# Feed-forward products of a two-block transformer kernel: lower gated rows multiplied right behind their gate, sums of the down sets moved into the first product, left buffers assigned anew

## The reference, cut to what matters

```python
D_FF = 2816
def swiglu_ffn(x, w_gate, w_up, w_down):          # x: 512 x 1024
    return (jax.nn.silu(x @ w_gate) * (x @ w_up)) @ w_down

x = x + 0.5 * swiglu_ffn(rmsnorm(x, ffn1_norm[l]), ffn1_w_gate[l], ffn1_w_up[l], ffn1_w_down[l])
x = x + hybrid_mixer(...)
x = x + 0.5 * swiglu_ffn(rmsnorm(x, ffn2_norm[l]), ffn2_w_gate[l], ffn2_w_up[l], ffn2_w_down[l])
x = rmsnorm(x, final_norm[l])
```

## Time and profile before

| | us |
|---|---|
| median of 3 runs (lowest to highest) | 1792.81 (1790.96 to 1795.54) |
| the profiled execution | 1793.75 |
| its span | 1791.9 |
| TensorE busy | 1728.6 (96%) |
| VectorE busy | 1009.5 (56%) |
| ScalarE busy | 711.6 (40%) |

### The profile page before, as it was taken

One profiled execution on the slowest core, in us unless ns is written; L12 is line 12 of the kernel. 1 busy time (PEld: TensorE's weight loads), 2 busy tenths in 40 slices (PEclk: granted clock), 3 DMA queues, 4 the chain that ended last, 5 costly groups with the idle time before them and its releaser, 6 DMA issues.

```text
span 1791.9 us, 21492 instructions
## 1 busy us (share of the span) xinstructions
PE 1728.6 (96%) x8703; PEld 1282.3 (72%) x8703; DVE 1009.5 (56%) x1491; ACT 711.6 (40%) x1146; POOL 78.9 (4%) x78
## 2 busy tenths in 40 slices
PE   7999999989999999999999999999999999999997
PEld 6878888875545454544577887897877887887896
DVE  4768865642333232323558756755487557756755
ACT  4556335442111111111335455454355435455452
POOL 0000000000000000000011110100000001110100
PEclk9999999999999999999999999999999999999999
DMA  6222225557999999999838897873202267897871
GB/s 215 93 71 71 95 83 176 192 193 281 422 421 421 421 421 421 421 421 421 318 106 203 196 210 182 179 191 117 95 24 83 95 163 183 197 213 176 172 186 59
DMA packets 117513, 385.75 MB, mean 215 GB/s; under 512 B 7088, under 2 KB 22592, under 8 KB 91424
## 3 DMA queue, kind: packets, MB, share of 16 engines
q1 hardware_dynamic: 88928, 318.33, 46.3%
q0 software_dynamic: 26176, 61.78, 18.7%
q10 hardware_dynamic: 2304, 4.20, 0.6%
HBM read 364.36 MB, written 6.29 MB: 207 GB/s over the span
## 4 chain that ended last, share of the span: by engine, by line
PE 79%; DVE 12%; ACT 6%; issue 1%; DMA 1%; POOL 0%; SPq 0%; DVEq 0%; ACTq 0%
PE PS L1509 12%; PE PS L1621 6%; PE PS L1623 6%; PE PS L1622 6%; PE PS L1542 6%; PE PS L1656 5%; PE PS L1658 5%; PE PS L1657 5%; DVE lo L2412 4%; PE PS L1660 3%; PE PS L1662 3%; PE PS L1661 3%; ACT hi L1965 2%; PE PS L1480 2%; PE PS L1481 2%; PE PS L1552 2%
## 5 line engine op out<-in xcount | busy, mean ns | idle before, releaser
L2412 DVE TENSOR_TENSOR lo<-raw,hi 128x1024 fp32r<-128x1024 f32 (+2 forms) x275 | 332.0, 1225 | 247.3 <-ACT hi L1965 243.3
L1965 ACT CAST hi<-raw 128x1024 fp32r<-128x1024 f32 (+2 forms) x277 | 286.8, 1060 | 229.6 <-PE PS L1623 146.3
L1621 PE MATMUL PS<-hi,xh_ffn 128*128 128x512 f32 (+1 forms) x320 | 118.1, 369 | 0.0
L1623 PE MATMUL PS<-hi,xl_ffn 128*128 128x512 f32 (+1 forms) x320 | 117.5, 367 | 0.0
L1622 PE MATMUL PS<-lo,xh_ffn 128*128 128x512 f32 (+1 forms) x320 | 117.5, 367 | 0.0
L1509 PE MATMUL PS<-raw,XG 128*64 128x512 f32 x352 | 117.1, 593 | 0.0
L2372 DVE TENSOR_TENSOR HF<-SG,PS 128x512 f32<-128x512 f32 x16 | 17.4, 1090 | 165.5 <-PE PS L1509 165.5
L2387 DVE SCALAR_TENSOR_TENSOR YL<-PS,SM,YH 128x512 fp32r<-128x512 f32 x30 | 21.1, 747 | 138.8 <-ACT YH L1948 138.8
L2395 DVE TENSOR_TENSOR x_sb<-x_sb,PS 128x512 f32<-128x512 f32 x128 | 78.1, 678 | 8.7 <-PE PS L1553 8.7
L1931 ACT COPY HT<-PS 128x512 f32<-128x512 f32 x16 | 9.4, 586 | 175.1 <-PE PS L1518 175.1
L1660 PE MATMUL PS<-xTh,hi 128*128 128x512 f32 x192 | 78.3, 408 | 0.4 <-DVE lo L2412 0.3
(11 more groups left out here) (520 smaller groups left out, 4220.6 us busy)
## 6 DMA issues: line engine op xcount, KB each, us to landing
raw<-in_w_in SPq DMA_DIRECT2D x26, 1024.0 KB, 5.2
rawz<-in_w_down_experts SPq DMA_DIRECT2D x25, 1024.0 KB, 11.1
raw<-in_w_up_experts SPq DMA_DIRECT2D x24, 1024.0 KB, 15.5
raw<-in_w_gate_experts SPq DMA_DIRECT2D x20, 1024.0 KB, 15.8
raw<-in_ffn_w_down SPq DMA_DIRECT2D x20, 1024.0 KB, 7.6
rawz<-in_w_up_experts SPq DMA_DIRECT2D x19, 1024.0 KB, 19.5
raw<-in_w_down_experts SPq DMA_DIRECT2D x16, 1024.0 KB, 12.4
rawz<-in_w_gate_experts SPq DMA_DIRECT2D x16, 1024.0 KB, 14.2
```

What stands on the lines that cost most here:

```text
L1621: e.matmul(o, xh[:, k, c], h[:, k, :], start=k == 0 and not more, stop=False, skip_group_check=more)
L1623: x = e.matmul(o, xl[:, k, c], h[:, k, :], start=False, stop=k == 3, skip_group_check=more)
L1965: e.copy(q.hi[:, a:b], q.raw[:, a:b]).then_inc(*a_hi((u, 0) if part == 0 else u))
L2412: e.tensor_tensor(q.lo[:, a:b], q.raw[:, a:b], q.hi[:, a:b].bitcast(F32), ALU.subtract).then_inc(*v_lo(key))
```

## The change: what it does

There are three parts, all in the feed-forward layers.

1. "hb" stands at the end of `behind[5]`'s gate steps instead of behind product 6, so before the split of left operand A11 and before the weight splits that `feed.take` and `feed.split_first` add around product 6. "ht" stands before product 0 of the next set, and ahead of the turns of rows 2 and 3, instead of behind product 0; only the turns of rows 0 and 1 (`upper`) stay behind it. The same holds before the plain down product, where "ht" also goes ahead and the turns of rows 0 and 1 stay.
2. In a down set the split of S2 and the read-out of product 0 (`seven_x`) stand behind product 0, with the sums S1 and S2 that are there already; and the weight unit of product 2 is split there too, ahead of the turns of rows 0 and 1. A12, S1, A22, S4 keep their places behind products 1 to 4.
3. The left operands of products 0 to 6 lie in LB0, LB1, LB0, LB2, LB1, LB0, LB2 instead of LB0, LB1, LB2, LB0, LB1, LB2, LB0, and the waits of their rounding are changed to fit: A12 now waits for product 0, S1 for product 1, A22 for product 2, S4 for product 3, and S2 for nothing in its own set.

```diff
-        ahead = []
+        ahead, upper = [], []
         if past:
-            ahead = turns(*past, (2, 3))
-            behind[0] = gates("ht", past) + turns(*past, (0, 1))
+            ahead = gates("ht", past) + turns(*past, (2, 3))
+            upper = turns(*past, (0, 1))
         if what[0] == "gu":
             p, cut = what[1:]
-            own = {1: ("R1",), 2: ("C11",), 3: ("R2", "sg", "R0"), 4: ("C22",), 5: ("C21", "sgb"), 6: ("hb",)}
+            own = {1: ("R1",), 2: ("C11",), 3: ("R2", "sg", "R0"), 4: ("C22",), 5: ("C21", "sgb", "hb")}
...
             behind[0].extend([("sum", pre, p, "S1"), ("sum", pre, p, "S2")])
-            for j, ws in ((1, ("A12", "S2")), (2, ("S1",)), (3, ("A22",)), (4, ("S4",))):
-                for w in ws:
-                    behind[j].extend(split_left(pre, p, w))
-            for j, js in ((1, (1,)), (2, (0,)), (3, (3,)), (4, (4,)), (5, (5,)), (6, (2, 6))):
+            for j, w in ((0, "S2"), (1, "A12"), (2, "S1"), (3, "A22"), (4, "S4")):
+                behind[j].extend(split_left(pre, p, w))
+            for j, js in ((0, (0,)), (1, (1,)), (3, (3,)), (4, (4,)), (5, (5,)), (6, (2, 6))):
                 behind[j].extend(("seven_x", pre, p, q, t) for q in js for t in range(2))
...
             S.extend(behind[j])
+            if j == 0:
+                if what[0] == "s":
+                    feed.split_to(feed.taken + 2)
+                S.extend(upper)
...
         if ui == 0:
-            S.extend(turns(*past, (2, 3)))
+            S.extend(gates("ht", past) + turns(*past, (2, 3)))
...
             elif i == 3:
-                S.extend(gates("ht", past) + turns(*past, (0, 1)))
+                S.extend(turns(*past, (0, 1)))
...
-        LEFT_H = [LB[i] for i in (0, 1, 2, 0, 1, 2, 0)]
+        LEFT_H = [LB[i] for i in (0, 1, 0, 2, 1, 0, 2)]
...
-                    if j >= 3:
-                        act.wait_ge(p_mm, ((n, "s", p), j - 3, 1))
+                    if j in (2, 4, 5, 6):
+                        act.wait_ge(p_mm, ((n, "s", p), {2: 0, 4: 1, 5: 2, 6: 3}[j], 1))
                     elif p:
-                        act.wait_ge(p_mm, ((n, "s", p - 1), (6, 4, 5)[j], 1))
+                        act.wait_ge(p_mm, ((n, "s", p - 1), {0: 5, 1: 4, 3: 6}[j], 1))
```

## The result

| | before | after |
|---|---|---|
| median, us | 1794.12 (4 runs, 1790.96 to 1795.54) | 1771.57 (4 runs, 1770.76 to 1773.71) |
| ratio | | 0.9879, 95% interval 0.9861 to 0.9896 |
| profiled execution, its span | 1793.75, 1791.9 | 1771.79, 1770.0 |

The forecast was 1768.3, between 1762 and 1777. The measured gain is 22.5 us between the medians, the forecast one 24.6. Lines above 700 have moved by three: 1594 is now 1597, 1621 to 1623 are 1624 to 1626, 2412 is 2415, 2488 is 2491.

A forecast was written before the change was run, and what follows sets the result against it. TensorE, 96% busy, was taken as the bound, so only earlier starts count. Gains of 17.4 + 5.7 + 1.5 = 24.6 us gave 1768.3 us against the median 1792.81, with an 8-in-10 range of 1762 to 1777.

The forecast's parts named there:

- Into the down sets: Gate-up set followed by down set, four places: 26.1 us instead of 30.63 to product 4, 17.4 us gained together.
- The new wait of product 2: In each of four down sets, TensorE waits 2.2 us for A12's rest before product 2.
- between the ends I take no fall: Down sets: clock stays up after the 2.2 us wait; a fall would cost up to 7.2 us more in all.
- R1: Rival: the clock falls in the new wait before product 2 of the down sets; 1775.5 us, chance 0.14.
- no wait, with under 0.2 to spare: Down sets: product 4 starts without waiting for product 3's read-out, under 0.2 us to spare.
- My two reference points: Idle times before turns: 3.64 us followed by a clock fall, 1.64 us without; 2.2 taken as nearer the latter.
- Gate-up set into gate-up set: Four places where a gate-up set follows another: 1.43 us gained each, 5.7 us together.
- Into the plain down product: Two places before the plain down product: gain 1.24 less 0.5 lost on turned rows, 0.75 each, 1.5 us together.
- R2: Rival: no new wait at product 2 of the down sets; 1759.5 us, chance 0.09.
- R3: Rival: VectorE bounds the whole down set, bringing back read-out waits and some wait at product 2; 1774 us, chance 0.11.
- R4: Rival: sums by adding DMAs become the wait, at T2 for product 3 in down sets; 1796 us, chance 0.03.
- R5: Rival: TensorE finds another reason to wait at the turns and the time stays; 1793 us, chance 0.04.

The follow-up runs named there:

- e3: Against the kernel before: down-set order and left buffers as in the change, "hb" and "ht" not moved; 1790.54 us, ratio 0.9974.
- e2: Against the kernel before: only "hb" moved earlier, "ht" stays behind product 0 of the next set; 1767.19 us, ratio 0.9844.
- e0: The whole changed kernel run again, nothing altered; 1772.16 us, ratio 0.9869 against the kernel before.
- e6: e7 plus, before the plain down product, turned rows split ahead of "ht" and first down weights split by halves; 1759.00 us, ratio 0.9804.
- e1: Against the kernel before: only "hb" and "ht" moved earlier, down sets and left buffers as before; 1765.75 us, ratio 0.9836.
- e7: e1 with the sum S4 one product later, behind the read-out of product 3; 1761.83 us, ratio 0.9818.

## Why the prediction was right, point by point

**Into the down sets.** "hb" in VectorE's pause, turns at once, product 0 at full clock: all as worked out: 26.1 us were forecast to product 4, and 26.25 and 26.23 were measured at the two places without a fall. The new wait of product 2 was put at 2.2 us on A12's rest, and is 1.93 to 2.04.

**The step that was mis-sized** is the bound "between the ends I take no fall" (R1, given 0.14). The clock fell at two of four places, 1.6 us each. Four stretches give 4.38, 2.71, 2.34 and 4.14, 13.6 us instead of 17.4: 3.2 of the 3.8 are the falls, 0.6 the start of product 4, put at "no wait, with under 0.2 to spare". It is 0.14 late each time: the last matmul of product 3 starts at 1000.80, so at the steady spacing product 4 would start at 1001.03, but it starts at 1001.17, released by the first half of the read-out, which ended at 1001.01:
```profile
1000.33 0.68 DVE L2529 SCALAR_TENSOR_TENSOR x_sb<-PS,x_sb 128x512 f32<-128x512 f32 x1
1001.13 0.19 PEld L1624 LDWEIGHTS PS<-hi,LB1h 128*128 128x128 f32 x1 [0.37 <-DVE x_sb L2529]
```
The four gains of the forecast, 4.5, 4.4, 4.1 and 4.3, also add up to 17.3 and not 17.4. My two reference points, 3.64 us with a fall and 1.64 without, bound nothing: a wait of 1.93 us had a fall and one of 3.59 (in e3) had none. I should have taken R1 as a thing that happens at some of the four places.

**Gate-up set into gate-up set.** From the last matmul of the old set to product 1 of the new one, the two 512-wide places give 1.43 and 1.41, the two 384-wide ones 1.45 and 1.43: 5.7 us, as forecast. e2 shows that "ht" is needed for part of it.

**Into the plain down product.** 0.75 each forecast; 0.60 and 0.59 measured. Both small new waits are where they were put. The one on the weights is 0.60 instead of 0.7, that on the turned rows 0.26 of idle time instead of 0.5; but it costs 0.55, since behind it the matmuls start later than the idle time alone explains, which I had left out. That "ht" before line 2460 adds delay is borne out by e2, where it stays behind the product and no wait on the turned rows is left.

**The sum.** 13.6 + 5.7 + 1.2 = 20.5 us inside the layers. The spans differ by 21.9: the first product of the first layer starts at 935.25 instead of 936.97, 1.7 us that the change has no part in (in e0 the same kernel starts it 1.4 us later again), and product 4 of gu(2,0) loses 0.4 in a wait on the copy RB. So the change itself brought 20.1 us of the 24.6 forecast in this pair of profiles, and 1.7 of what the spans show is luck.

**R2 and R3** are out by the four equal waits and the absent read-out wait. **R4**, the adding DMAs: at the first place they are issued at 977.5 and 979.7 and land 8.7 and 11.5 us later, with no wait of ScalarE for them in a down set. The box on the "DVE blocks DMA" trap in the Trainium skill ("SBUF — State Buffer") says that GpSimd can't write the descriptors of its DMAs while VectorE runs an op in a two-port mode. The same two took 8.5 and 10.8 us before, so the fuller VectorE shows no slowing of several times here; whether its ops run in such a mode no run shows. In a gate-up set such a DMA does begin to show: in gu(2,0) ScalarE waits for the sum T4 and makes the copy RB late for product 4, by 0.23 us of idle time in the change and in e6, 0.6 in e1, 0.95 in e7.
```profile
ACT hi L1965 <- DMA raw<-raw: 2.9, 1, 2.9
```
**R5** is out. What I did not ask was whether the gain needed parts 2 and 3. The numbers for it stood in the prediction: I had found that the moved split and read-out "take the idle time of VectorE, but in front of A12", and called it part of the change's price, without working out the queue in the old order. e1 shows that this order leaves product 2 no wait at all.

## What to carry to other kernels

Where an engine is stopped by one result, look at what stands ahead of its producer in that producer's queue: one entry moved up into a pause was worth 27 of 29 us here (e2 against e1). Then, before filling the pauses that the move leaves, write down for each engine which entry TensorE waits for next and put nothing in front of it: parts 2 and 3 put such entries ahead of A12 and lost 6 us, and moving one sum back behind the next read-out won 4. Reckon a wait of 2 us at 2 to 3.6, since a fall came behind some of these waits and not behind others of the same length.

## What the runs showed of the hardware that was not expected

The granted clock can fall after an idle time of 1.93 us (0.66 over the next 5 us; two of four places in two profiles had a fall, one of four in a third), and can stay at 1.00 after 3.59 us: in e3_down_only the second of the four places kept it, while the three others, with the same wait, read 0.58, 0.67 and 0.64. TensorE's timeline there and the window behind it:
```profile
1103.58 0.39 PE L1627 MATMUL PS<-hi,XS4l 128*128 128x512 f32 x1
1107.56 1.26 PE L1598 MATMUL PS<-C,RB 128*128 128x128 f32 x8 [3.59 <-DVE RB L2521]
```
```profile
1107.50:1111.60 4.10, 4.04 (x21) 3.35 (x22) 4.07 (x5) 1.18 (x2) 1.31 (x2) 1.00 0.85 132
```
The length of an idle time alone does not tell which it will be. What else counts, the moment or something else, is open.
